# Hybrid RWKV-7 / RG-LRU / PEER decoder step: the next pair's rows prepared inside the pair before it, and four edits that go with that

## The reference, cut to what matters

```python
h  = x * (1 + sc1) + sh1                       # modulation by silu(c) @ w_ada
P  = h @ w_in                                  # RWKV columns and RG-LRU columns
m  = concat(rwkv7(P_A), rglru(P_B)) @ w_out    # 16 RWKV heads x 64, 16 LRU blocks x 64
x  = layernorm(ALPHA * x + (1 + g1) * m)
h2 = x * (1 + sc2) + sh2
x  = layernorm(ALPHA * x + (1 + g2) * peer(h2))

# rwkv7, per head, with kk normalised to length 1 per head
p = p + (shifted - p) * mu_shift               # token shift
S = S * w + (S @ -kk) (kk * a)^T + v k^T       # state, 64 x 64
y = S r ;  y = (y - mean) / sqrt(var + eps) * lnx_w + lnx_b ;  out = (y + (r.k.r_k) v) * g

# peer, per row and per head: 16 best of 128 x 128 expert pairs
gate = softmax(sv) ;  act = gelu(peer_u[e] . h2) ;  out += gate * act * peer_v[e]
```

## Time and profile before

| what | value |
|---|---|
| time of 3 runs | 4527.43 us median, 4522.81 to 4528.02 |
| the profiled execution's own time | 4525.16 us |
| span of its records | 4523.6 us |
| mean granted clock of PE | 0.919 of full speed |
| PE busy | 4074.8 us (90%) |
| DVE busy | 3036.7 us (67%) |

### The profile page before, as it was taken

How to read it: one execution, slowest core, us unless ns; L and a number is a source line. 1 busy time by engine, 2 the same in 40 slices (tenths; PEclk the granted TensorE clock), 3 DMA queues, 4 the chain that set the end, 5 groups by cost and what they waited for, 6 DMA issues and landing times. The chain is left out here.

```text
span 4523.6 us, 72560 instructions
## 1 busy us (share of the span) xinstructions
PE 4074.8 (90%) x29289; PEld 3856.0 (85%) x29289; DVE 3036.7 (67%) x3968; ACT 1459.4 (32%) x2056; POOL 1461.1 (32%) x775
## 2 busy tenths in 40 slices
PE   5897889889889866997998999999997999999997
PEld 4896777778778755996998999999997999999996
DVE  1564443543543543335998888888877999999996
ACT  1343221221221211114222444444423343444433
POOL 0331312222222211001346534444442444444441
PEclk6998888988988866998999999999998999999998
DMA  8221122212212112312235999999998999999994
GB/s 359 81 86 59 68 75 76 84 65 80 88 65 80 68 54 80 144 65 90 83 124 206 348 383 375 383 372 389 380 376 326 367 388 373 373 386 379 382 355 170
DMA packets 214284, 982.51 MB, mean 217 GB/s; under 512 B 21953, under 2 KB 101953, under 8 KB 106561
## 3 DMA queue, kind: packets, MB, share of 16 engines
q1 hardware_dynamic: 92256, 524.19, 30.4%
q0 software_dynamic: 57984, 409.37, 23.2%
q10 hardware_dynamic: 63840, 46.15, 3.1%
HBM read 917.54 MB, written 62.09 MB: 217 GB/s over the span
## 5 line engine op out<-in xcount | busy, mean ns | idle before, releaser
L93 PE MATMUL PS<-first_HH,tail_WH 128*128 128x352 f32 (+1 forms) x3072 | 975.6, 318 | 68.5 <-DVE first_HL L1696 34.1
L95 PE MATMUL PS<-first_HH,tail_WL 128*128 128x352 f32 (+1 forms) x3072 | 959.3, 312 | 0.0
L94 PE MATMUL PS<-first_HL,tail_WH 128*128 128x352 f32 (+1 forms) x3072 | 958.0, 312 | 0.0
L93 PE MATMUL PS<-dn_BH,tail_WH 128*128 128x352 f32 x2048 | 669.4, 327 | 35.7 <-DVE dn_BL L2270 21.3
L95 PE MATMUL PS<-dn_BH,tail_WL 128*128 128x352 f32 x2048 | 660.4, 322 | 0.0
L94 PE MATMUL PS<-dn_BL,tail_WH 128*128 128x352 f32 x2048 | 658.8, 322 | 0.0
L93 PEld LDWEIGHTS PS<-first_HH,tail_WH 128*128 128x128 f32 x3072 | 583.9, 190 | 74.4 <-issue 48.6
L2246 POOL DMA_INDIRECT dn_VR<-in_v_rows,tail_EI x192 | 430.8, 2244 | 607.3 <-DVEq L2289 568.9
L1998 POOL DMA_INDIRECT up_UR<-in_u_rows,tail_EI x192 | 423.5, 2206 | 516.7 <-DVEq L2080 482.4
L94 PEld LDWEIGHTS PS<-first_HL,tail_WH 128*128 128x128 f32 x3072 | 585.0, 190 | 0.5
L95 PEld LDWEIGHTS PS<-first_HH,tail_WL 128*128 128x128 f32 x3072 | 583.2, 190 | 0.0
(11 more groups left out here) (401 smaller groups left out, 7852.7 us busy)
## 6 DMA issues: line engine op xcount, KB each, us to landing
tail_WR<-in_peer_u SPq DMA_DIRECT2D x128, 1024.0 KB, 9.0
tail_WR<-in_peer_v SPq DMA_DIRECT2D x128, 1024.0 KB, 8.1
mix_RING<-in_w_ada SPq DMA_DIRECT2D x88, 1024.0 KB, 4.8
mix_RING<-in_w_in SPq DMA_DIRECT2D x38, 1024.0 KB, 4.9
tmp_z<-up_ZB ACTq DMA_DIRECT2D x128, 176.0 KB, 7.3
tmp_gd<-up_STG ACTq DMA_DIRECT2D x22, 1024.0 KB, 18.2
dn_GG<-tmp_gd SPq DMA_DIRECT2D x16, 1408.0 KB, 10.6
dn_ZI<-tmp_z SPq DMA_DIRECT2D x128, 176.0 KB, 6.2
```

The costliest lines, as they stand in the source:

```text
L93: nc.tensor.matmul(out, r32(wh), r32(xh), start=first, stop=False)
L94: nc.tensor.matmul(out, r32(wh), r32(xl), start=False, stop=False)
L95: return nc.tensor.matmul(out, r32(wl), r32(xh), start=False, stop=last)
```

## The change

There are five edits.

- A. The first two projections of RWKV pair 0 are done in the LRU phase, one before and one after its last `gates`, with their loads, high and low parts; the RWKV phase starts with the third.
- B. `prep` is cut in two. `prep_rows` (the token shift and the decay, L1264 to L1279 of before) of pair i+1 runs inside `post` of pair i, between the mean's subtraction and the wait for the variance. The third weight tile's low part goes from POOL to DVE (`low_third`), after `post`.
- C. PE's loop over pairs 0 to 5 is written out. DVE gets `prep_rows(0)` and two `low_third` ahead of its loop.
- D. In the up phase EARLY is 6: POOL makes low parts up to number 36 before it waits for the experts, then 2 fetches and 3 low parts with one fetch between each; DVE does three dots before and three after the softmax. The wait for the keys stands behind the second query tile.
- E. The down phase's memsets go from DVE to POOL, ahead of its first fetch.

```diff
@@ phase_lru
             project(3, 1, 1)
+            project(4, 0, 0)
             gates(3, 1)
+            project(4, 0, 1)
@@ phase_rwkv, PE
-            for which in range(3):
-                project(pe, 0, which)
+            pe.sem_inc(proj_done, 2)
+            pe.sem_inc(slot_used, 2)
+            project(pe, 0, 2)
...
-            with pe.Fori(0, NPAIR - 2) as i:
+            for i in range(NPAIR - 2):
                 pair(i, True, True)
@@ phase_rwkv, POOL
-                if ahead2:
-                    low(pool, i + 2, 2)
                 pool.wait_ge(so_out, 32 * i + 32)
@@ phase_rwkv, DVE
-        def prep(dve, i):
+        body = slice(1, W1)
+
+        def prep_rows(dve, i):
...
             V.tensor_tensor(DT[:, body], DT[:, body], KX[:, body], ALU.mult)
+            dve.drain().then_inc(wd_used, 1)
+
+        def prep(dve, i):
+
+            V = nc.vector
             dve.wait_ge(ss_done, i + 1)
             V.tensor_scalar(halves(NR[:, body]), PS[:, 0:2, 0:TPH], 1e-24, None, ALU.max)
             dve.drain().then_inc(ss_ready, 1)
-            dve.sem_inc(wd_used, 1)
...
+        def low_third(dve, i):
+
+            dve.wait_ge(wh_ready, 3 * i + (2 - 1))
+            nc.vector.tensor_tensor(r32(LOW[2]), RAW[2], HIGH[2], ALU.subtract).then_inc(wl_third, 1)
...
             dve.drain().then_inc(yc_ready, 1)
+            if ahead:
+                prep_rows(dve, i + 1)
             dve.wait_ge(sd_ready, i + 1)
...
+                post(dve, i, ahead)
+                if ahead2:
+                    low_third(dve, i + 2)
+
+            low_third(dve, 0)
+            prep_rows(dve, 0)
+            low_third(dve, 1)
+            with dve.Fori(0, NPAIR - 2) as i:
+                pair(i, True, True)
+            pair(NPAIR - 2, True, False)
+            pair(NPAIR - 1, False, False)
@@ phase_up, POOL
-            tiles = EARLY // 2
-            for i in range(2, NP - tiles):
+            for i in range(2, NP - 3):
                 low(i)
             pool.wait_ge(ei_ready, 1)
-            for n in range(tiles):
-                fetch(2 * n)
-                fetch(2 * n + 1)
-                low(NP - tiles + n)
-            for j in range(EARLY, PICKS):
+            fetch(0)
+            for n in range(3):
+                fetch(n + 1)
+                low(NP - 3 + n)
+            for j in range(4, PICKS):
                 fetch(j)
@@ phase_down
+            nc.gpsimd.memset(YS[:], 0.0)
+            nc.gpsimd.memset(YR[:], 0.0)
+            nc.gpsimd.memset(YA[:], 0.0)
+            pool.drain().then_inc(cleared, 1)
...
-            V.memset(YA[:], 0.0)
-            V.memset(YS[:], 0.0)
-            V.memset(YR[:], 0.0)
```

More of the change, by code:

```diff
@@ L386, in _ @@
                     store_rows(2 * j + odd)
-            sp.wait_ge(slot_used, 15)
-            sp.dma_start(SLOT[2], io["w_in"][0]).then_inc(g["X_IN"], 16)
+            for k in range(2):
+                sp.wait_ge(slot_used, 15 + k)
+                sp.dma_start(SLOT[2 + k], io["w_in"][8 * k]).then_inc(w_in[2 + k], 16)
             for i in (6, 7):
@@ L530, in _ @@
                     high_of(j + 1, odd, 1)
+            high_of(4, 0, 0)
             tile(6, 0)
+            high_of(4, 0, 1)
             tile(7, 1, last=True)
@@ L553, in _ @@
                 low(16 + k, k, k)
+            for k in range(2):
+                low(18 + k, k, 2 + k)
         @block.vector
@@ L753, in phase_rwkv @@
      sd_ready, post_done, mix_free, so_ready, so_free, sp_ready, sp_free, pp_used, wd_used,
-     ag_used) = (m.sem(x) for x in (
+     ag_used, wl_third) = (m.sem(x) for x in (
         "cleared slot_used proj_done proj_ev gk_free banks_idle act_rows sq_ready ss_done ss_ready "
@@ L758, in phase_rwkv @@
         "r2_ready gk_done gk_read gk_ready s_done s_ready yy_done yt_ready mean_done yc_ready ysq_ready var_done "
-        "sd_ready post_done mix_free so_ready so_free sp_ready sp_free pp_used wd_used ag_used").split())
+        "sd_ready post_done mix_free so_ready so_free sp_ready sp_free pp_used wd_used ag_used wl_third").split())
     PC0, PC1 = 1 + SEQ, W1
@@ L791, in load_low @@
                 sp.dma_start(WLR[:], io["w_lr"][i]).then_inc(wlr_in, 16)
-            load_tile(0, 1)
             load_low(0)
@@ L843, in project @@
                 if half == 0:
-                    pe.wait_ge(wl_ready, 3 * i + which + 1)
+                    if which == 2:
+                        pe.wait_ge(wl_third, i + 1)
+                    else:
+                        pe.wait_ge(wl_ready, 2 * i + which - 1)
                 cols = slice(TPH * half, TPH * half + TPH)
@@ L876, in high @@
             if which == 1:
-                act.wait_ge(y_in, 16 * i + 16)
+                act.wait_ge(y_in, 16 * i)
             else:
-                act.wait_ge(x_in, 32 * i + (16 + 8 * which))
+                act.wait_ge(x_in, 32 * i + 8 * which)
             nc.scalar.activation(r32(HIGH[which]), RAW[which], ACT.Copy).then_inc(wh_ready, 1)
         def low(pool, i, which):
-            pool.wait_ge(wh_ready, 3 * i + which + 1)
+            pool.wait_ge(wh_ready, 3 * i + which - 1)
             nc.gpsimd.tensor_tensor(r32(LOW[which]), RAW[which], HIGH[which], ALU.subtract).then_inc(wl_ready, 1)
@@ L894, in evacuate @@
                     act.wait_ge({0: pp_used, 3: wd_used, 4: ag_used}[which], i)
-                src = PS[:, BANKS[which]:BANKS[which] + 2, 0:TPH]
+                bank = (0, 2)[which] if hi == 2 else BANKS[which]
+                src = PS[:, bank:bank + 2, 0:TPH]
                 dst = halves((PP[:, which] if which < 3 else (WD, AG, GN)[which - 3])[:, 1:W1])
@@ L1145, in _ @@
             A = nc.scalar.activation
-            high(act, 0, 0)
-            high(act, 0, 1)
             act.wait_ge(cleared, 1)
-            evacuate(act, 0, 0, 1)
+            evacuate(act, 0, 0, 2)
             high(act, 0, 2)
-            evacuate(act, 0, 1, 4)
+            evacuate(act, 0, 2, 4)
             high(act, 1, 0)
@@ L1188, in _ @@
             G = nc.gpsimd
-            for k in range(2):
-                low(pool, 0, k)
             pool.wait_ge(cleared, 1)
@@ L1198, in _ @@
             load_states(0)
-            low(pool, 0, 2)
-            for k in range(3):
+            for k in range(2):
                 low(pool, 1, k)
@@ L1255, in _ @@
             pair(NPAIR - 1, False, False)
-        def prep(dve, i):
+        body = slice(1, W1)
+        def prep_rows(dve, i):
             V = nc.vector
-            body = slice(1, W1)
             dve.wait_ge(rows_in, i + 1)
@@ L1422, in dve_samples, with post @@
             dve.drain().then_inc(so_ready, 1)
-        def post(dve, i):
+        def post(dve, i, ahead):
             V = nc.vector
@@ L1459, in _, with pair @@
             dve.sem_inc(banks_idle, 1)
-            with dve.Fori(0, NPAIR) as i:
+            def pair(i, ahead, ahead2):
                 prep(dve, i)
@@ L1464, in _ @@
                 dve_samples(dve, i)
-                post(dve, i)
+                post(dve, i, ahead)
[8 more added lines that the diff above has]
+            pair(NPAIR - 1, False, False)
             for lo, hi in ((2, 3), (4, 6)):
@@ L1764, in batches_of @@
     return range(max(0, n - UA), min(GATES, n - UA + 1))
-EARLY = 12
+EARLY = 6
 def dots_of(n):
@@ L1875, in tables @@
                 mm.then_inc(tab_done, 1)
-            pe.wait_ge(keys_in, 16)
             query(0)
@@ L1880, in _ @@
                 query(i + 1)
+                if i == 0:
+                    pe.wait_ge(keys_in, 16)
                 scores(i)
@@ L1962, in _ @@
                 act.dma_start(io["z"][n], ZB[:, n % 2]).then_inc(z_out[n % 2], 16)
-                if n == UA - 6:
+                if n == UA - 4:
                     act.wait_ge(ex_in, 1)
@@ L2298, in _ @@
                     rest(a - 1)
+            dve.wait_ge(cleared, 1)
             for v in range(NV):
```

## The result

The changed kernel takes 4461.31 us (median of 4 runs, 4454.39 to 4480.48); before, 4527.73 us in 4 runs of the same series. The ratio is 0.9859, 95% interval 0.9826 to 0.9892: the change makes the kernel 1.4% faster. The profiled execution has a span of 4459.7 us, 63.9 us less than before.

A forecast was written before the change was run, and what follows sets the result against it. It took PE as the engine to follow, its RWKV waits sitting at the boundaries. Terms −37.3 − 4.3 − 4.4 − 16.5 + 4 = −58.5 us led from 4527.4 to 4468 us, range 4447 to 4489.

The forecast's parts named there:

- four stretches that were put at nothing: Forecast 0 for the modulation, the pairs' steps and samples, output projection with first query tile, and down phase with last norm.
- the signs that the prediction named: Included boundaries of 34 to 35 us, no "issue" wait at pairs 1 to 6, 104 up-phase tiles not over 905 us.
- Boundaries, −37.3: RWKV boundaries 0-1 to 5-6: without branch and with projection at full clock, each takes 34.3 us; −37.3 us for six.
- ACT's square: At the boundaries, ACT's square for the head sum: lateness taken as 0; a table load would add 1 us or so, six times.
- Code: PE's code grows by five copies of a pair; long straight code was costed at nothing.
- Boundary 6-7, −4.3: RWKV boundary 6-7, bound by DVE: rows moved ahead let the factors end at 1652.6 instead of 1657.06; −4.3 us.
- the start, −4.4: RWKV phase start: two projections moved into the LRU phase, gates later but 2.0 us long, one projection left; −4.4 us.
- The first part, −16.5: Up phase's first tiles: fewer low parts behind POOL's stop, new wait for DVE's low part; 2496.0 against 2512.5, −16.5 us.
- The second term: Up phase's 104 later tiles: six more gathers and dots there cost +4 us, between 0 and 16.8.
- rival 1: Up phase gives it all back: six late gathers cost 16.8 instead of 4 us, total 4481 us; chance 0.20.
- The keys' wait, 0: Up phase start: the wait for the keys moves behind a second tile whose own load must come first; worth nothing.

The follow-up runs named there:

- e2: Changed kernel with PE's loop over pairs 0 to 5 put back, all else as changed; 4501.1 us, ratio to before 0.9953.
- e1: Kernel before with only PE's loop over pairs written out; 4524.32 us, ratio to before 1.0012.
- e3: Changed kernel with the whole up phase of before (EARLY 12, order of gathers, place of the keys' wait); 4466.45 us, ratio to before 0.9881.
- e5: Changed kernel where every eighth gather of the up phase fetches 64 columns of other rows instead of 2048; leaves out needed work; 4433.35 us.
- e6: Changed kernel where every eighth dot of the up phase multiplies 64 columns instead of 2048, all gathers in full; leaves out needed work; 4472.85 us.
- e4: Changed kernel with the third weight tile's low part made by POOL again instead of DVE; 4464.52 us, ratio to before 0.9853.

## Why the prediction was right, and what was mis-sized

*What bounds the kernel* was read rightly: the boundaries were where the time was. That the sum came as near as it did (−58.5 forecast, −63.9 measured in the profiles) is in part luck: the later tiles cost 9.2 us more than forecast, the boundaries gave 4.6 us more, and another 11.3 us came from four stretches that were put at nothing, 4.4 of them chance. Of the signs that the prediction named, two were just missed: a boundary takes 33.5 us and not 34 to 35, and the 104 tiles 905.57 us and not at most 905. From 4527.4 the sum of its terms comes to 4468.9 us, not 4468.

*Boundaries, −37.3, measured −41.9.* The steps of the working hold: no branch, a projection at full clock, DVE and ACT in time. ACT's square, which I took at 0 to 1 us late, is made at 631.62, 5 us before PE wants it, since the copy ahead of it came 1.6 us earlier behind the variance and no branch of ACT's shows between the two, only a table load of 1.28 us. The 4.6 us more are 0.76 us at each of the six. About 0.5 of it lies ahead of the head sum: the first product (624.61) starts 0.37 us before the variance's end (matmuls overlap, and the profile models their ends), where I took 0.26 us behind it, while the projection took 12.54 and not 12.40 us. The other 0.26 lies behind the second head sum: with the loop, `project_low` shows two pauses of 0.21 us in each of the five pairs, before and in e2, and written out none. What the prediction didn't say, and e1 and e2 show, is that B and C are worth little alone: 1.4 us in five boundaries for the rows (e2), and none for the written-out loop (e1). It counted the branch and the clock as C's and used B only as a condition; by its own numbers C alone should have been costed with DVE's rows at 646.73.

*Code.* Written out, the pairs show no wait of the kind "issue" longer than 0.26 us (gaps of 0.2 to 0.3 us stood before, too, beside the five long ones that the prediction counted). The Trainium skill ("Runtime: NRT & Kernel Launch", section "Instruction fetch mechanics") has branches, not long code, as what costs; e2's five gaps of up to 4.4 us, back with the loop, agree.

*Boundary 6-7, −4.3, measured −4.7* (33.19 to 28.45 us), and *the start, −4.4, measured −3.8*: the gates came later and took 2.07 us as supposed, and the one projection left took 14.7 us where I took 15.1.

*Up phase.* The first part, −16.5, measured −15.4, by the mechanism described: DVE's low part, behind the sixth dot, is the new wait. The 1.1 us less are in the sum's making: it set the end of that low part against the evacuation of tile 23, two different events. The second term is the step that was mis-sized: I took +4 us for six late gathers, "nearer to the lower end", from DVE's 69 us of waits. It is +13.2 in the two profiles, and some 8 to 14 in the others (e3), nearer to the upper bound of 16.8. That was rival 1 in its mechanism, and it came true. The waits of DVE on gathers say little here, for they are not where PE stands: in the 104 tiles PE waits for the tables' operands from ACT 8.8 us before, 16.5 after and 2.8 in e5, and for the tiles' low parts 6.1, 6.4 and 0.4. That these waits come from the tables' and the tiles' transfers fits e5, but the profile doesn't name what ACT waited for. A warning was in the profile: the DMA engines were busy 0.98 of that stretch before, and PE 876.87 of 892 us. I weighed 375 GB/s against the Trainium skill's 425 for a core alone ("HBM Reference", section "Specifications (TRN2)") and saw room; no run here reached that rate: in slices of some 112 us, the most is 396 GB/s (e6), and in the 104 tiles the engines were busy 0.98 of the time at 376.

*The keys' wait, 0, measured −1.7.* Moved behind the second query tile, it no longer holds PE: the first query product waits 6.35 us, now for POOL's signal at the phase's start, and not 8.06 for the keys. This is most of the 2.4 us in the table's row of the output projection and the first query tile, a term that the prediction put at nothing.

*E* was worth nothing that shows, as forecast: PE's idle stretch at the down phase's start is 19.83 us, 19.13 before.

## What to carry to other kernels

Where two waits of one engine lie on top of each other, each edit alone measures as nothing; look for what is late next before you judge it, and try them together. Before moving transfers out of a stall into a later stretch, read what is free there: with the DMA engines busy 0.98 and PE 877 of 892 us, 5.5 MB moved in came back as some 8 to 14 us. The busy share alone doesn't say what binds (0.97 in e5); a run with fewer bytes does. After each gain read the wait that ends the stretch now: here it was a wait for more than PE needed, and one line was worth 2 us a pair.

## What the runs showed of the hardware that was not expected

An idle stretch of 4 to 6 us on PE costs 1.2 to 2.7 us more in the 13 us of products behind it, whether it is a branch (1.2 to 2.6 us in before and e2; 0.80 and 0.82 granted in the projection at 0-1) or a wait for ACT (1.6 us behind 4.81, 2.5 to 2.7 behind 6.2 in e1; 0.50 in the head sum, then 0.86). The price of such a wait is therefore a quarter to two thirds more than the wait itself.

Beside a low part of POOL a DVE instruction took 4.56 us (0.18 by itself; L1442 before) and 4.68 us (0.73 by itself; e4). Not every one is held up: a pair of TENSOR_REDUCE of the up phase took 2.88 us beside a low part and 2.88 without. In the up phase DVE's choice of experts ends 370.7 us after the phase's first load, 362.8 before: POOL no longer stands still at its end, and a pair of DVE instructions there takes 7.15 us and not 2.90. e3, in which POOL stands still again for 14.40 us, shows 364.0 and 2.89 us, so it is the up phase's edits that cost these 7 us.
